# Tile 0's down rows fetched as two halves each from the stream of weights, without copies of the rows in DRAM

## What is computed

```python
def peer_ffn(h, wq, subkeys, u, v):
    q = (h @ wq).reshape(B, T, PEER_HEADS, 2, PEER_QDIM // 2)
    s = jnp.einsum('bthpd,pnd->bthpn', q, subkeys)
    s_top, i_top = lax.top_k(s, 16)
    cand = s_top[..., 0, :, None] + s_top[..., 1, None, :]
    cand_idx = i_top[..., 0, :, None] * 128 + i_top[..., 1, None, :]
    best, pos = lax.top_k(cand.reshape(B, T, 8, 256), 16)
    experts = jnp.take_along_axis(cand_idx..., pos, axis=-1)   # 8 heads x 16 = 128 experts a token
    gates = jax.nn.softmax(best, axis=-1)
    ...
        a = jnp.einsum('td,tkd->tk', hx, u[e])
        return jnp.einsum('tk,tkd->td', g * jax.nn.gelu(a), v[e])
```

## Time and profile before

| | us |
|---|---|
| median of 3 runs without a profile | 3818.95 |
| lowest and highest of them | 3815.77, 3824.24 |
| the profiled execution | 3855.64 |
| its span, first to last instruction | 3853.8 |
| PE busy | 3758.7 (98%) |
| DVE busy | 2394.1 (62%) |
| POOL busy | 2049.0 (53%) |
| ACT busy | 1435.7 (37%) |

### The profile page before, as it was taken

The page is one execution under the profiler, slowest core; times in us unless marked ns, Lnnn a source line. Parts: engine busy times, 40 slices in busy tenths (PEclk is TensorE's granted clock), DMA queues, the critical chain, the costliest instruction groups (busy, mean ns, idle before and its releaser), DMA issues.

```text
span 3853.8 us, 47176 instructions
## 1 busy us (share of the span) xinstructions
PE 3758.7 (98%) x17288; PEld 3044.7 (79%) x17288; DVE 2394.1 (62%) x3962; ACT 1435.7 (37%) x2059; POOL 2049.0 (53%) x1486
## 2 busy tenths in 40 slices
PE   7999999999999999999999999999999999999999
PEld 5767878788878878888877678787877888788887
DVE  5736558977812237888766363489677222488887
ACT  4537533333323333333345373323323333333332
POOL 2432333477766537777434223335777666476772
PEclk9999999999999999999999999999999999999999
DMA  7656463576665459999847554436766754899995
GB/s 291 221 186 209 163 240 106 202 255 226 225 228 197 147 207 377 373 389 370 295 155 247 177 193 143 156 113 238 241 230 208 245 173 135 284 376 380 370 364 209
DMA packets 395414, 919.33 MB, mean 239 GB/s; under 512 B 64352, under 2 KB 136928, under 8 KB 395136
## 3 DMA queue, kind: packets, MB, share of 16 engines
q1 hardware_dynamic: 288384, 715.37, 53.6%
q0 software_dynamic: 69632, 134.82, 9.9%
q10 hardware_dynamic: 37248, 67.33, 4.7%
HBM read 844.33 MB, written 257.56 MB: 286 GB/s over the span
## 4 chain that ended last, share of the span: by engine, by line
PE 85%; DVE 8%; DMA 2%; issue 2%; ACT 1%; POOL 1%; another core or an unknown queue 0%; SPq 0%; ACTq 0%; DVEq 0%; POOLq 0%
PE ps L1074 16%; PE ps L1076 16%; PE ps L1075 16%; PE ps L1092 9%; PE ps L1093 9%; PE ps L1094 9%; DMA g_in<-expert_gate 1%; PE ps L1349 1%; PE ps L1353 1%; PE ps L1351 1%; PE ps L1316 1%; PE ps L1330 1%; DMA raw<-in_stream_dram 1%; POOL acts L1015 1%; PE ps L1306 1%
## 5 line engine op out<-in xcount | busy, mean ns | idle before, releaser
L1026 POOL DMA_INDIRECT expert_gate<-gate_v,gate_i x768 | 865.2, 1127 | 413.1 <-issue 197.2
L1010 POOL TENSOR_TENSOR w_lo<-raw,w_hi 128x1024 fp32r<-128x1024 f32 x178 | 443.5, 2492 | 906.9 <-ACT w_hi L620 906.9
L1074 PE MATMUL ps<-h_hi,w_hi 128*128 128x512 f32 x1776 | 702.5, 396 | 20.9 <-ACT gel L944 8.7
L1075 PE MATMUL ps<-h_hi,w_lo 128*128 128x512 f32 x1776 | 695.2, 391 | 0.0
L1076 PE MATMUL ps<-h_lo,w_hi 128*128 128x512 f32 x1776 | 694.9, 391 | 0.0
L620 ACT ACTIVATE w_hi<-raw 128x1024 fp32r<-128x1024 f32 x380 | 401.1, 1056 | 747.8 <-PE ps L1076 440.9
L944 ACT ACTIVATE gel<-ps 128x512 f32<-128x512 f32 x256 | 153.1, 598 | 828.5 <-PE ps L1076 546.1
L1015 POOL DMA_INDIRECT acts<-expert_act,e_act x256 | 352.7, 1378 | 170.9 <-DMA expert_act<-gel 93.5
L1035 POOL DMA_INDIRECT down<-expert_down,e_row x256 | 329.9, 1289 | 212.4 <-DVE y L1962 87.8
L1074 PEld LDWEIGHTS ps<-h_hi,w_hi 128*128 128x128 f32 x1776 | 334.5, 188 | 101.9 <-issue 26.6
L1074 PE MATMUL ps<-h_hi,w_hi_up 128*128 128x512 f32 x992 | 390.6, 394 | 16.4 <-issue 14.9
(11 more groups left out here) (291 smaller groups left out, 6949.2 us busy)
## 6 DMA issues: line engine op xcount, KB each, us to landing
raw<-in_stream_dram SPq DMA_DIRECT2D x648, 512.0 KB
expert_down<-in_stream_dram SPq DMA_DIRECT2D x256, 512.0 KB
expert_act<-gel ACTq DMA_DIRECT2D x256, 256.0 KB
raw_more<-in_stream_dram SPq DMA_DIRECT2D x128, 512.0 KB
expert_gate<-zeros SPq DMA_DIRECT2D x96, 512.0 KB, 6.1
a_in<-expert_act SPq DMA_DIRECT2D x128, 384.0 KB
g_in<-expert_gate SPq DMA_DIRECT2D x128, 384.0 KB
expert_gate<-gate_v,gate_i POOLq DMA_INDIRECT x768
```

The source lines that it names most:

```text
L1010: pool.tensor_tensor(w_lo[:, s, :], raw[:, b, :], w_hi[:, s, :].bitcast(F32), ALU.subtract).then_inc(lo_ready, 1)
L1026: pool.indirect_dma_start(out=gate_d[l], out_offset=bass.IndirectOffsetOnAxis(ap=gate_i[:, tt, h, c:c + 1], axis=0), in_=gate_v[:, tt, h, ...
L1074: pe.matmul(o, sta_hi[:, w], mov_hi[:, c, :], start=c == 0, stop=False)
L1075: pe.matmul(o, sta_lo[:, w], mov_hi[:, c, :], start=False, stop=False)
```

## The change

The copies, `expert_down`, `copies_by` and the semaphore `down_stored` go. `fetch_row` now reads the stream itself, seen as rows of 512 elements (`half_rows`): for each k it issues two indirect DMAs, one for each half of the rows, into the two halves of the same buffer. The halves of an expert's row lie 4 units, that is 1024 of these rows, apart. `e_row` holds two row numbers for each pick, and `half_row` works them out on DVE from the two key numbers: 2 j + (i and 1) + 256 (i >> 1) + 1024 (i >> 3), and the place of the layer's first down unit. DVE's wait for a row is now for 32 instead of 16 steps of the semaphore. `e_row`, `gate0` and `acts0` get other places in SBUF.

```diff
--- before.py
+++ after.py
@@ -99,15 +99,6 @@
 SLOT = [{u: p - NK * _l for u, p in PLACE[_l].items()} for _l in range(DEPTH)]
 
 
-COPIES_M = 32
-
-
-def copies_by(l, p):
-
-    first, last = PLACE[l]["w", U_SQ] - START[l], PLACE[l]["w", U_MIXB] - START[l]
-    return COPIES_M * min(max(p - first + 1, 0), last - first) // (last - first)
-
-
 COLUMN_UNITS = ([(m, "act") for m in range(U_Q, U_V)] + [(m, "act") for m in range(U_SQ, U_MIXA)]
                 + [(m, "act" if held(m) % 2 == 0 else "dve") for m in range(U_MIXA, U_OUT)]
                 + [(m, "dve") for m in range(U_WQ, U_U)] + [(m, "act") for m in range(U_U, U_VE)])
@@ -212,7 +203,7 @@
     gate_d = [nc.dram_tensor(f"expert_gate{l}", (NK * P * DSEQ, 1), F32, kind="Internal").ap() for l in range(DEPTH)]
     gate_units = [g.rearrange("(i j t) o -> i j (t o)", i=NK, j=P) for g in gate_d]
     zero_d = nc.dram_tensor("zeros", (P, 512), F32, kind="Internal").ap()
-    down_d = [nc.dram_tensor(f"expert_down{l}", (NK * P, D), F32, kind="Internal").ap() for l in range(DEPTH)]
+    half_rows = stream.rearrange("n p (k c) -> (n p k) c", k=2)
     base = (nc.sbuf_base + 31) // 32 * 32
 
     def at(name, kb, shape, dt=F32):
@@ -304,9 +295,9 @@
     w_lo_up2 = at("w_lo_up2", Z + 44, [P, 1024], F32R)
     w_lo_up3 = at("w_lo_up3", Z + 108, [P, 1024], F32R)
     e_act = at("e_act", Z + 24, [P, PICKS], U32)
-    e_row = at("e_row", Z + 24.5, [P, PICKS], U32)
-    gate0 = at("gate0", Z + 25, [P, PICKS])
-    acts0 = at("acts0", Z + 25.5, [P, PICKS])
+    e_row = at("e_row", Z + 24.5, [P, 2, PICKS], U32)
+    gate0 = at("gate0", Z + 25.5, [P, PICKS])
+    acts0 = at("acts0", Z + 31, [P, PICKS])
     gate_r = at("gate_r", Z + 26, [P, DT, PH, TOPK])
     gate_v = at("gate_v", Z + 28, [P, DT, PH, TOPK])
     gate_i = at("gate_i", Z + 29.5, [P, DT, PH, TOPK], U32)
@@ -380,7 +371,7 @@
         out_ready, out_stored, down_lo = sem("out_ready"), sem("out_stored"), sem("down_lo")
         tile_done, row_tile = sem("tile_done"), sem("row_tile")
         x_half, half_sq, xn_act = sem("x_half"), sem("half_sq"), sem("xn_act")
-        down_stored, row_added = sem("down_stored"), sem("row_added")
+        row_added = sem("row_added")
         acts_got = [sem(f"acts_got{g}") for g in range(PH)]
         down_loaded = [sem(f"down_loaded{u}") for u in range(RING)]
         down_got = [sem(f"down_got{b}") for b in range(VB)]
@@ -462,14 +453,6 @@
                 else:
                     sp.wait_ge(down_lo, l * NK + n - RING + 1)
                 sp.dma_start(down_raw(n), stream[N_ADA1 + PLACE[l]["w", U_VE] + n]).then_inc(down_loaded[n % RING], 16)
-
-            def copy_down(l, n):
-
-                unit = stream[N_ADA1 + PLACE[l]["w", U_VE] + n].rearrange("p (k c) -> p k c", k=2)
-                g, dh, q = n // 8, n // 4 % 2, n % 4
-                e = g * 1024 + q * 256
-                sp.dma_start(down_d[l][e:e + 256, dh * 512:dh * 512 + 512].rearrange("(k p) c -> p k c", k=2), unit
-                             ).then_inc(down_stored, 16)
 
             def clear_gates(l, n):
 
@@ -490,8 +473,6 @@
                         else:
                             sp.wait_ge(ada_used, ada_count(l, k))
                     load(N_ADA1 + START[l] + p, slot % RAW)
-                    for n in range(copies_by(l, p - 1) if p else 0, copies_by(l, p)):
-                        copy_down(l, n)
                     for n in range(clears_by(l, p - 1) if p else 0, clears_by(l, p)):
                         if l == 0 and n == 0:
                             sp.wait_ge(zeros_stored, 16)
@@ -569,8 +550,6 @@
                 load_listed(l, queries, queries + RAW)
                 for m in range(U_WQ + 2 * RAW, U_U + 124):
                     load_split(l, m, m % RAW)
-                    if 0 <= m - U_U < NK - COPIES_M:
-                        copy_down(l, COPIES_M + m - U_U)
 
                 def load_pair(pair, b):
                     src = bass.ds(pair * 2, 2)
@@ -1032,9 +1011,10 @@
 
                 if k >= VB:
                     pool.wait_ge(row_added, l * PICKS + k - VB + 1)
-                pool.indirect_dma_start(out=down[k % VB][:], out_offset=None, in_=down_d[l],
-                                        in_offset=bass.IndirectOffsetOnAxis(ap=e_row[:, k:k + 1], axis=0)
-                                        ).then_inc(down_got[k % VB], 16)
+                for dh in range(2):
+                    pool.indirect_dma_start(out=down[k % VB][:, dh * 512:dh * 512 + 512], out_offset=None, in_=half_rows,
+                                            in_offset=bass.IndirectOffsetOnAxis(ap=e_row[:, dh, k:k + 1], axis=0)
+                                            ).then_inc(down_got[k % VB], 16)
 
             for l in range(DEPTH):
                 for m in range(U_U):
@@ -1051,7 +1031,6 @@
                     if put_after(n) > put_after(n - 1):
                         pool.wait_ge(unit_used, used(l, U_U + put_after(n)))
                     put_gate(l, n)
-                pool.wait_ge(down_stored, (l + 1) * NK * 16)
                 for s in range(2):
                     pool.wait_ge(gel_stored[s], 16 + (l + 1) * (NK // 2) * 16)
                 for k in range(TOPK):
@@ -1884,9 +1863,27 @@
                                                   scalar=float(DSEQ), in1=shift[:], op0=ALU.mult, op1=ALU.add))
                     dve.tensor_copy(gate_i[:, :, hs, :], gate_f[:, :, hs, :])
                     own = slice(32 * g, 32 * g + 32)
-                    dve.tensor_copy(e_row[:, own], e_id[:, 0, :])
+                    half_row(own)
                     step(dve.tensor_scalar(e_act[:, own], e_id[:, 0, :], float(SEQ), const[:, C_TOKEN:C_TOKEN + 1],
                                            ALU.mult, ALU.add))
+
+                def half_row(own):
+
+                    key_i, pair_n, block_n, odd = (half_i[:, 32 * b:32 * b + 32] for b in range(4))
+                    pair_f, block_f, odd_f = (half_f[:, 32 * b:32 * b + 32] for b in range(1, 4))
+                    row = half_f[:, 0:32]
+                    step(dve.tensor_copy(key_i, picked[:, 0, 0:32]))
+                    dve.tensor_scalar(pair_n, key_i, 1, None, ALU.logical_shift_right)
+                    dve.tensor_scalar(block_n, key_i, 3, None, ALU.logical_shift_right)
+                    step(dve.tensor_scalar(odd, key_i, 1, None, ALU.bitwise_and))
+                    step(dve.tensor_copy(half_f[:, 32:128], half_i[:, 32:128]))
+                    step(dve.scalar_tensor_tensor(out=row, in0=picked[:, 1, 0:32], scalar=2.0, in1=odd_f, op0=ALU.mult,
+                                                  op1=ALU.add))
+                    step(dve.scalar_tensor_tensor(out=row, in0=pair_f, scalar=256.0, in1=row, op0=ALU.mult, op1=ALU.add))
+                    step(dve.scalar_tensor_tensor(out=row, in0=block_f, scalar=1024.0, in1=row, op0=ALU.mult, op1=ALU.add))
+                    base = (N_ADA1 + PLACE[l]["w", U_VE]) * 2 * P
+                    for dh in range(2):
+                        dve.tensor_scalar(e_row[:, dh, own], row, 1.0, float(base + dh * 1024), ALU.mult, ALU.add)
 
                 def weigh(g):
 
@@ -1954,7 +1951,7 @@
                 def add_row(k):
 
                     row, w, o = down[k % VB][:], gate0[:, k:k + 1], y0[:] if k % 2 else even
-                    dve.wait_ge(down_got[k % VB], 16 * (l * len(range(k % VB, PICKS, VB)) + k // VB + 1))
+                    dve.wait_ge(down_got[k % VB], 32 * (l * len(range(k % VB, PICKS, VB)) + k // VB + 1))
                     if k < 2:
                         dve.tensor_scalar(o, row, w, None, ALU.mult).then_inc(row_added, 1)
                     else:
```

## The result

The changed kernel takes 3989.85 us (median of 4 runs, 3985.61 to 3999.27) beside 3817.36 us (3813.48 to 3824.24) for the kernel before: a ratio of 1.0453 [1.0429, 1.0478], 172.5 us slower. The forecast was 4010, range 3920 to 4090. The profiled execution took 3999.3 us, with a span of 3997.5 against 3853.8.

A forecast was written before the change was run, and what follows sets the result against it. POOL was to replace PE as the down stage's bound: +214 for fetches, -27 for copies, +3.6 for row numbers, +191 us in sum; 4046 us profiled, 4010 us without a profile, range 3920 to 4090.

The forecast's parts named there:

- What becomes the bound: Down stage: POOL, with 32 us to spare, becomes the bound instead of PE; DVE waits for rows, PE for DVE.
- The price of an issue: POOL's fetches in the down stage: 0.95 us undisturbed plus 0.30 us behind, whatever is moved; half a row pays it whole.
- The end at which the excess stays tied to DVE's work: POOL's down-stage period: 0.795 us a row of excess added to 3.75 us, giving 4.55 us a row, +187 us.
- the form I took: POOL's down-stage period: the excess over 0.95 us falls with DVE's busy share, giving 4.67 us a row.
- The estimate worked out from it: Down-stage issues under the port-lock rule: 0.95 + 0.36 + 0.30 = 1.61 us each, 4.82 us a row, +247 us.
- +107 us a layer for the fetches: Down stage: row 112 added at 1988.1 instead of 1881.31 with a 4.67 us period; +214 us for two layers.
- -27 us for the copies: Up stages: three quarters of 36 us come back when the DRAM-to-DRAM copies go, bounds 10 and 36.
- What they can give back is what PE lacks in the four disturbed stretches: Up stages: stretches of 100 us hold 415, 387, 423 and 388 matmuls instead of 443; 159 missing, 36 us.
- +3.6 us for the row numbers: Added small DVE instructions, 1.8 us a group; only each layer's first group holds PE, near 765 us; at most 7.
- Hidden issues (3803): Rival for the down stage: three issues take 3.75 us, PE's own pace, leaving the copies' gain; 8%.
- the DMA engines as the bound (4172): Rival for the down stage: 2 KB packets cost as much as 4 KB ones, 5.2 us a row, +188 us a layer; 5%.
- the clock: Rival for the down stage: PE's gaps halve its clock to 1.2 GHz, 460 us more a layer, near 4720; 3%.

The follow-up runs named there:

- chip 2: Both kernels timed once more, unedited, on another chip: before 3820.88 us, changed 3984.17 us, ratio 1.0434.
- the 4-byte fetch: Kernel before without copies, one 4 KB fetch a row plus a second indirect DMA of 4 bytes a partition: 3974.82 us, ratio 1.0412.
- short additions: Changed kernel with DVE adding only 64 of the 1024 columns of each row from the third on: 3926.92 us, ratio 1.0290.
- chip 12: Chip where the kernel before took 3854.73 us; without its copies it took 3849.01 us there, ratio 0.9988.

## Why the prediction was right, and where it was wrong

**What becomes the bound: right.** POOL's 32 us of room in the stage were gone with the second fetch. POOL issues back to back (402.0 of 403 us), its waits for additions are gone but for the last rows, additions wait for rows, and the whole loss lies where it was put, in the two down stages.

**The price of an issue: right.** "The price is thus that of an instruction with 128 addresses, whatever it moves": 1231 ns for 4 KB, 1189 ns for 4 bytes. The period was put at 4.67 between 4.55 and 4.88. Measured: 4.59 and 4.63 in the first trace, 4.58 and 4.55 on chip 2, 4.53 and 4.55 with the 4-byte fetch. The end at which the excess stays tied to DVE's work (4.55) was nearer than the form I took. With short additions the period was 4.29, so it does follow DVE. By the Trainium skill, "SBUF — State Buffer", section on SBUF's two separate sides, the engine that loses the shared port pair waits until the other's instruction ends. The estimate worked out from it, half a DVE instruction for each issue that meets one and 4.82 us a row, was too much here.

**+107 us a layer for the fetches: mis-sized.** Measured: 85.3 and 88.9 in the first pair of traces, 80.8 and 75.5 on chip 2. Three things, layer 1 of the first pair:
- The period: 112 x (4.67 - 4.59) = 9 us.
- The row's latency. I kept row 0's 8.0 us for row 112. Row 0's is 8.76 now, row 112's 1958.80 - 1953.44 = 5.36: 3.4 us.
- The tail. I let the loss at row 112 stand until the end of the layer; 94.0 - 85.3 = 8.7 us come back (7.6, 8.8 and 9.0 in the other three). In the kernel before DVE works two units, 2 x 4.08 = 8.2 us, ahead of PE; while POOL is the bound PE runs up against DVE, and when the fetches get cheaper, fewer units are left to PE behind each row. The size fits; no run tested it apart.

**-27 us for the copies: wrong.** The failed step is "What they can give back is what PE lacks in the four disturbed stretches". Most of what PE lacks stayed without copies on the chip that has the stalls (109 of 159 matmuls), and nothing was lacking with copies on one that hasn't (443). The copies are worth 5.7 us on the first and nothing measurable on a second. The mechanism was wrong too: "ACT's gelu needs the store of an earlier one to have landed" is true of the program, but the waits of 12.91 and 14.06 us end with PE's count of finished units, and no long wait on record ends with a store. A sign was in the numbers: the profiled execution lay 36.7 us above the median, about the size of the 36 us of stalls. I explained it as a fixed 1% and scaled it away. Against a trace without stalls they cost 36.6 us, so the whole of it was the stalls, which the timed runs didn't have to give back. The rule cited there (the Trainium skill, "DMA: Bandwidth & Descriptors", section on queues, rings and completion order) is about a store's semaphore behind other writes. It was taken to give the copies the whole 36 us; it doesn't bear on these waits, which are not for a store.

**+3.6 us for the row numbers: right as a wait, not measurable as time.** The wait grew by 1.6 to 1.7 us a layer; the runs gave -1.0 us.

**The sum.** +191 was put, 172.5 measured. Two misses of opposite sign lie behind the nearness: the fetches cost 156 to 174 in the traces instead of 214, the copies gave 0 to 6 instead of 27.

**The rivals.** Hidden issues (3803) falls by the period, the DMA engines as the bound (4172) by their share of 0.87 and by the 4-byte fetch, which costs as much. Of the clock a part came true. PE's wait of 6.55 us comes in units of two rows, and the clock behind some of these falls; timeline and stretch of the changed kernel:

```profile
1568.07 0.80 PE L1071 MATMUL ps<-w_hi_more,g_hi 128*128 128x512 f32 x1 [6.55 <-DVE w_lo_more L1947]
...
1560.00:1580.00 20.00, 13.45 (x52) 10.54 (x51) 11.64 (x12) 3.81 (x4) 16.01 (x14) 0.83 0.85 296
```

Over the stage the clock is 0.96. PE catches up since POOL is slower, and this term costs nothing that the period doesn't already hold.

**What stays open.** Why PE's count of finished units comes late in the up stage on chip 12, and in the prediction's trace, and not on the others; and whether POOL's puts, the only other traffic at that time, have part in it, for no run without them was made on a chip with the stalls. The copies may have a part in them: in the middle of the two up stages the stalls cost 36.6 and 35.2 us in the two traces with copies, and 26.7, 20.9 and 32.5 us in the three without, one trace for each kernel.

## What to carry to other kernels

Count GpSimd's indirect DMAs, not their bytes: here each costs 0.95 us alone, 1.2 to 1.4 beside a busy DVE, and 0.30 us to the next; to fetch a row in two halves is to pay twice, and the room on that queue in that stage says whether it hurts. If a profiled execution is longer than the timed median by as much as its stalls add up to, suspect that the timed runs don't have these stalls, and take no credit for removing them. Before a wait for several semaphores is put down to one, look for a second engine that is released at the same time: the one semaphore that both wait for is the likely one. A bound that moves to another engine for part of a stage is partly paid back at its end, by as much lead as the waiting engine had in hand.

## What was not expected of the hardware

- The same kernel takes 3855 us on chip 12 and 3817 to 3821 us in the other three sets of runs. The traces put the difference into the middle of the up stages, where PE's count of finished units reaches ACT late and ACT waits up to 14.06 us, while the DMA engines are almost idle (share 0.02).
- A second run of 2 KB in a unit's load instead of one of 4 KB cost little: 3857.81 against 3849.01 us for 256 units, about 9 us.
- 512 KB copies from DRAM to DRAM, 256 of them, cost nothing measurable and 5.7 us when hidden, at a DMA share of 0.71 instead of 0.43.
- Single waits of 6.5 us let TensorE's clock fall (0.83 from 1560 to 1580 us), where a stretch of 4 us with gaps of about 1 us kept 1.00.
